# A two-layer transformer kernel on one Trainium2 core: one regular timetable for the 192 modulation adds in place of hand-set places

## The reference

```
mod = jax.nn.silu(c) @ w_ada[l] + b_ada[l]          # (1, 2048) @ (2048, 12288)
shift_a, scale_a, gate_a, shift_f, scale_f, gate_f = jnp.split(mod, 6, axis=-1)
h = rms_norm(x, g_attn_pre[l]) * (1.0 + scale_a[:, None]) + shift_a[:, None]
...                                                 # projections, two attentions, w_o
x = x + gate_a[:, None] * rms_norm(mixed, g_attn_post[l])
h = rms_norm(x, g_ffn_pre[l]) * (1.0 + scale_f[:, None]) + shift_f[:, None]
ff = (jax.nn.silu(h @ w_gate[l]) * (h @ w_up[l])) @ w_down[l]
x = x + gate_f[:, None] * rms_norm(ff, g_ffn_post[l])
```

## Time and profile before

| | |
|---|---|
| median of 3 runs | 2756.78 us (2755.45 to 2757.07) |
| the profiled execution's own time | 2756.78 us, of which 2755.0 us are the span from the first to the last instruction |
| PE busy | 2618.4 us, 95% of the span |
| DVE busy | 1839.9 us, 67% |
| ACT busy | 1313.6 us, 48% |
| DMA | 558.31 MB, mean 203 GB/s |
| PE on the chain that ended last | 91% |
| mean granted TensorE clock | 0.966 of full |
| L1297, 180 of the 192 adds | 1278 ns each |

### The profile page before, as it was taken

The page is one execution under the profiler, slowest core; times in us unless marked ns, Lnnn a source line. Parts: engine busy times, 40 slices in busy tenths (PEclk is TensorE's granted clock), DMA queues, the critical chain, the costliest instruction groups (busy, mean ns, idle before and its releaser), DMA issues.

```text
span 2755.0 us, 36683 instructions
## 1 busy us (share of the span) xinstructions
PE 2618.4 (95%) x14858; PEld 2265.9 (82%) x14858; DVE 1839.9 (67%) x2620; ACT 1313.6 (48%) x2021; POOL 0.2 (0%) x4
## 2 busy tenths in 40 slices
PE   7999769999999999999998999869799999999998
PEld 6887658888888888888887888658688888888886
DVE  5566455677878788788788546774666656655555
ACT  5456254445544444444445443455554444444454
POOL 0000000000000000000000000000000000000000
PEclk9999689999999999999999999969899999999999
DMA  7555006677878878878785654304377757655552
GB/s 256 192 197 170 1 31 215 206 251 276 294 241 277 285 259 293 271 268 305 254 277 186 199 187 154 117 0 138 107 244 239 235 185 231 227 183 195 187 189 86
DMA packets 329857, 558.31 MB, mean 203 GB/s; under 512 B 13526, under 2 KB 158128, under 8 KB 329176
## 3 DMA queue, kind: packets, MB, share of 16 engines
q1 hardware_dynamic: 299312, 451.58, 49.8%
q10 hardware_dynamic: 30376, 104.39, 10.9%
HBM read 551.72 MB, written 4.19 MB: 202 GB/s over the span
## 4 chain that ended last, share of the span: by engine, by line
PE 91%; DVE 4%; ACT 2%; issue 1%; ACTq 0%; DVEq 0%
PE ps L441 56%; PE ps L442 29%; PE ps L521 1%; PE ps L458 1%; PE ps L532 1%; PE ps L509 1%; DVE sm_cols L1419 1%; PE ps L728 1%; PE ps L636 0%; ACT wh L829 0%; DVE wl L1281 0%; PE ps L476 0%; PE ps L650 0%; PE ps L497 0%; DVE ts L1792 0%
## 5 line engine op out<-in xcount | busy, mean ns | idle before, releaser
L441 PE MATMUL ps<-hs,wh 128*128 128x512 f32 x4816 | 1685.0, 395 | 18.6 <-issue 12.3
L1281 DVE TENSOR_TENSOR wl<-raw,wh 128x1024 fp32r<-128x1024 f32 x856 | 1039.5, 1223 | 766.4 <-ACT wh L829 763.4
L829 ACT ACTIVATE wh<-raw 128x1024 fp32r<-128x1024 f32 x856 | 899.1, 1059 | 1134.6 <-PE ps L442 1102.0
L442 PE MATMUL ps<-hs,wl 128*128 128x256 f32 x4816 | 1345.2, 279 | 0.0
L441 PEld LDWEIGHTS ps<-hs,wh 128*128 128x128 f32 x4816 | 903.8, 188 | 232.4 <-issue 15.7
L442 PEld LDWEIGHTS ps<-hs,wl 128*128 128x128 f32 x4816 | 909.1, 189 | 1.2 <-issue 1.2
L441 PE MATMUL ps<-ff,wh 128*128 128x512 f32 x1728 | 606.7, 396 | 0.0
L442 PE MATMUL ps<-ff,wl 128*128 128x256 f32 x1728 | 484.8, 281 | 0.0
L441 PEld LDWEIGHTS ps<-ff,wh 128*128 128x128 f32 x1728 | 324.1, 188 | 76.5
L442 PEld LDWEIGHTS ps<-ff,wl 128*128 128x128 f32 x1728 | 326.7, 189 | 0.0
L855 ACT ACTIVATE te<-ps 128x256 f32<-128x256 f32 x445 | 132.9, 383 | 9.8 <-PE ps L442 6.2
(11 more groups left out here) (238 smaller groups left out, 1314.6 us busy)
## 6 DMA issues: line engine op xcount, KB each, us to landing
raw<-w_down SPq DMA_DIRECT2D x108, 1024.0 KB
raw<-w_in SPq DMA_DIRECT2D x80, 1024.0 KB
raw<-w_up SPq DMA_DIRECT2D x64, 1024.0 KB
ada_w<-w_ada ACTq DMA_DIRECT2D x96, 512.0 KB, 5.1
ada_more<-w_ada ACTq DMA_DIRECT2D x96, 512.0 KB, 5.8
raw<-w_gate SPq DMA_DIRECT2D x88, 512.0 KB
raw<-w_up SPq DMA_DIRECT2D x88, 512.0 KB
raw<-w_in SPq DMA_DIRECT2D x68, 512.0 KB
```

Source lines behind the costliest of these rows:

```text
L441: nc.tensor.matmul(ps[0:m, b, :], wh[:, slot, w0:w0 + m], x2, start=k == 0, stop=False)
L442: mm = nc.tensor.matmul(ps[0:m, b, 0:T], wl[:, slot, w0:w0 + m], x2[:, 0:T], start=False, stop=end)
L829: nc.scalar.activation(wh[:, h % WH_SLOTS, :], raw[:, slot, HALF * q:HALF * (q + 1)], ACT.Copy).then_inc(wh_ready, 1)
L1281: nc.vector.tensor_tensor(wl[:, h % WH_SLOTS, :], raw[:, slot, HALF * q:HALF * (q + 1)], wh[:, h % WH_SLOTS, :], ALU.subtract).then_inc(wl ...
```

## The change

The hand-set places are replaced by one pattern for all 12 chunks. A chunk now spans four steps. Counted as (step of the chunk, half), its adds stand after (-1,6), that is half 6 of the step before, then (0,0) (0,2) (0,4) (0,6), (1,0) (1,2) (1,4) (1,6), (2,0) (2,2) (2,4) (2,6), (2,7), (3,0) and (3,1). The sum stands after half 3 of step 3, the close after the feed of half 5. The chunks lie in LGY's gate steps 4 to 7, the four steps of L4, the 32 of LF1 (an up chunk and a down chunk in each quarter), and steps 1 to 8 of LF2's first part, where chunks 10 and 11 now both lie. The sum writes bank 0 of the next step's banks, not bank 3, and the wait for the close moves from that step's fourth tile to its start; one wait is added ahead of the sums of squares after LF1.

```
--- before.py
+++ after.py
@@ -78,32 +78,31 @@
 
 
 
-
-
-def ada_places(panel, *halves):
-
-    return [2 * panel + h for h in halves]
-
-
-ADA_PLACES = [ada_places(LGY.panel + 24, 1, 4, 7, 10, 13, 16, 19, 22, 25, 28, 31, 34, 37, 40, 43, 46),
-              ada_places(L4.panel, 4, 5, 7, 8, 10, 12, 14, 15, 16, 18, 20, 22, 24, 26, 28, 30)]
-ADA_STEPS = [(L4.panel, L4.step, 2), (LF1.panel, LF1.step, 2)]
-for c in range(4):
-    up, t_up = LF1.panel + 32 * c, LF1.step + 8 * c
-    ADA_PLACES += [ada_places(up, 4, 5, 7, 11, 13, 15, 19, 21, 23, 27, 29, 31, 32, 33, 34, 35),
-                   ada_places(up + 20, 0, 1, 3, 5, 6, 8, 10, 11, 13, 14, 16, 17, 18, 20, 21, 22)]
-    ADA_STEPS += [(up + 16, t_up + 4, 6), (up + 32, t_up + 8, 2)]
-for c in range(2):
-    ADA_PLACES.append(ada_places(LF2.panel + 4 + 44 * c, *[8 * s + h for s in range(8) for h in (2, 5)]))
-    ADA_STEPS.append((LF2.panel + 36 + 44 * c, LF2.step + 9 + 11 * c, 2))
-ADA_ADDED = {ADA_PLACES[m][k]: 16 * m + k for m in range(12) for k in range(16)}
+ADA_STEPS = ([LGY.panel + 6 * s for s in range(4, 8)] + [L4.panel + 4 * s for s in range(4)]
+             + [LF1.panel + 4 * s for s in range(32)] + [LF2.panel + 4 * s for s in range(1, 9)])
+ADA_PLACES = [(-1, 6)] + [(s, h) for s in range(3) for h in (0, 2, 4, 6)] + [(2, 7), (3, 0), (3, 1)]
+ADA_SUMS, ADA_CLOSES = 3, 5
+
+
+def ada_half(chunk, step, h):
+
+    first = ADA_STEPS[4 * chunk] if step < 0 else ADA_STEPS[4 * chunk + step]
+    if step < 0:
+        first -= 6 if chunk == 0 else 4
+    return 2 * first + h
+
+
+ADA_ADDED = {ada_half(m, *ADA_PLACES[k]): 16 * m + k for m in range(12) for k in range(16)}
 ADA_LAST = 2 * LF2.panel + 2
 ADA_LOADED = {2 * (LGY.panel + 12) + 1: [0, 1, 2, 3], ADA_LAST: [160, 161, 162, 163]}
 for at_half, n in ADA_ADDED.items():
     if n + 4 < 160 or 164 <= n + 4 < 192:
         ADA_LOADED.setdefault(at_half + 1, []).append(n + 4)
-ADA_SUMMED = {2 * ADA_STEPS[m][0] + ADA_STEPS[m][2]: m for m in range(12)}
-ADA_BEFORE = {ADA_STEPS[m][0] + 4: m for m in range(12)}
+ADA_SUMMED = {ada_half(m, 3, ADA_SUMS): m for m in range(12)}
+ADA_CLOSED = {ada_half(m, 3, ADA_CLOSES): m for m in range(12)}
+ADA_BEFORE = {ADA_STEPS[4 * m + 3] + 4: m for m in range(12)}
+ADA_BANKS = ([LGY.step + 15, L4.step + 4] + [LF1.step + 4 * m + 4 for m in range(8)]
+             + [LF2.step + 5, LF2.step + 9])
 RAW_SLOTS = 4
 PANEL_INC = 64
 N_VECTORS = 15
@@ -423,6 +422,8 @@
 
 
                 pe.wait_ge(tile_summed, 4 * (t + dt) + 4)
+                if p + dp in ADA_BEFORE:
+                    pe.wait_ge(ada_read, ADA_BEFORE[p + dp] + 1)
                 last = len(tiles) - 1
                 for h in range(2 * panels):
                     slot = (2 * p + h) % WH_SLOTS
@@ -431,8 +432,6 @@
                     pe.wait_ge(wl_ready, 2 * (p + dp) + h + 9)
                     for n, (c0, m) in enumerate(tiles):
                         b = bank(t, n)
-                        if h == 0 and n == 3 and p + dp in ADA_BEFORE:
-                            pe.wait_ge(ada_read, ADA_BEFORE[p + dp] + 1)
                         for kk in range(2):
                             k = 2 * h + kk
                             end = k == 4 * panels - 1
@@ -455,7 +454,7 @@
                 pe.wait_ge(tile_summed, 4 * (t + dt) + 4)
                 pe.wait_ge(ada_used, 16 * chunk + 20)
                 for j in range(8):
-                    mm = nc.tensor.matmul(ps[:, bank(t, 3), j:j + 1], ada_acc[:, j * P:(j + 1) * P], ones[:, 0:1],
+                    mm = nc.tensor.matmul(ps[:, bank(t, 0), j:j + 1], ada_acc[:, j * P:(j + 1) * P], ones[:, 0:1],
                                           start=True, stop=True)
                 mm.then_inc(ada_summed, 1)
 
@@ -715,6 +714,7 @@
             ffn_chunk(0, first=True)
             for c in range(1, 4):
                 ffn_chunk(c)
+            pe.wait_ge(ada_read, 10)
             norm_sums(NORM_A, L7.step)
 
 
@@ -1281,10 +1281,10 @@
                 nc.vector.tensor_tensor(wl[:, h % WH_SLOTS, :], raw[:, slot, HALF * q:HALF * (q + 1)],
                                         wh[:, h % WH_SLOTS, :], ALU.subtract).then_inc(wl_ready, 1)
                 at_half = h + 2 * dp - 4
-                if at_half in ADA_SUMMED:
-                    ada_close(ADA_SUMMED[at_half])
                 if at_half in ADA_ADDED:
                     ada_add(ADA_ADDED[at_half] // 16, ADA_ADDED[at_half] % 16)
+                if at_half in ADA_CLOSED:
+                    ada_close(ADA_CLOSED[at_half])
 
             def ada_add(chunk, k):
 
@@ -1300,7 +1300,7 @@
 
             def ada_close(chunk):
                 dve.wait_ge(ada_summed, chunk + 2)
-                nc.vector.tensor_tensor(mod[:, 8 * chunk:8 * chunk + 8], ps[:, bank(ADA_STEPS[chunk][1] + 1, 3), 0:8],
+                nc.vector.tensor_tensor(mod[:, 8 * chunk:8 * chunk + 8], ps[:, bank(ADA_BANKS[chunk], 0), 0:8],
                                         bada[:, 8 * chunk:8 * chunk + 8], ALU.add).then_inc(ada_read, 1)
 
             def total(t, dt, n, dst, m=P, inc=1):
```

## The result

The changed kernel takes 2802.2 us (median of 6 runs, 2782.8 to 2806.4), the kernel before 2756.9 in the same comparison (2754.1 to 2767.8). All ratios here, with their 95% intervals, are over the fast runs alone, and one run of the kernel before in a later comparison, 3308.1 us at a granted clock of 0.735, is left out. The ratio is 1.0139 (1.0115 to 1.0162), some 38 us; the two medians lie 45 us apart, more than that, since four of the six runs of the kernel before took 2754 to 2757 us and two 2766 to 2768. The forecast was 2771.6 with a range of 2763 to 2782: the sign was right, but of the 38 to 45 us it had 15. The profiled execution took 2795.55 us, its span is 2793.8 us against 2755.0.

A forecast was written before the change was run, and what follows sets the result against it. TensorE was taken to set the time, new waits being paid in full. 2756.8 us plus 14.8 of stalls at the sums, with pace and clock at 0, gave 2771.6 us; range 2763 to 2782.

The forecast's parts named there:

- TensorE sets the time, a new wait is paid in full; what is only moved costs nothing.: Feed-forwards: TensorE busy 95% of the span, so only its new waits cost; moved adds, loads and closes cost 0.
- The wait for `ada_read`: At the next step's start: the moved wait costs nothing, as the close stands after half 5's feed.
- The stalls.: TensorE waits at sums for the last add: up chunks 11.8, LF2 1.9, L4 0.9, down 0.2; together 14.8 us.
- The full clock through the stalls: At the new waits ahead of sums: the granted clock stays full, adding 0 us to the forecast.
- a rival at 20 in 100: Up chunks' stalls and sums: the clock falls, 1.5 to 2.1 us each, 6 to 8 together, giving 2779; 20 in 100.
- The pace.: TensorE's two speeds, 22.19 and 22.61 us a step, with borders at sums: taken as 0, range -7 to +8 us.
- a slow half: Half of a step at TensorE's slower pace, 0.053 us longer; 197 counted between sums, 10.5 us.
- the rule that each sum turns the pace over as before: LF1 would have 4 x 32 slow halves for 109, LF2 32 for 88: 2.0 us less.
- The rival on the other side: All slow stretches vanish as the sums move: -10.5 us, giving 2761.1, +0.16%; 7 in 100.
- The rival with late feeds: Up steps: denser adds delay `wl` for half 4, up to 1 us in each of 16 steps, giving 2785; 4 in 100.
- the marks I named: Profile signs: longest four waits 2.9 to 3.0 us, last add at +13.9; wrong if new clock falls between 760 and 1485 us.
- The step of 27.0 us: Quarter 1's steps with a sum: 22.19 + 1.8 for the sum + 3.0 for the stall = 27.0 us.

The follow-up runs named there:

- sum5: The changed kernel with its 12 sums after half 5 of their step, not half 3; all adds stay. 2762.9 us, ratio 0.9997 to the kernel before.
- add25: The changed kernel with one add of each chunk moved from after half 7 of the third step to after half 5. 2772.9 us, ratio 1.0039.
- before_s5: The kernel before with the sums of its four up chunks after half 5 of the first down step, not half 6. 2778.3 us, ratio 1.0054.
- after_b: The changed kernel, unaltered, run and profiled again. 2801.9 us, ratio 1.0133 to the kernel before.
- busy12: The changed kernel with 12 extra unused matmuls ahead of the sum's wait in each of the four up chunks. 2787.2 us, ratio 1.0082.
- busy_all: The changed kernel with extra unused matmuls ahead of the sum's wait: 12 in each up chunk, 4 in each LF2 chunk. 2789.7 us, ratio 1.0083.
- before_b: The kernel before, unaltered, profiled once more in another execution. 2763.3 us in one run.
- before_c: The kernel before, unaltered, profiled as a third draw, on the same chip as the second. 2769.5 us in one run.

## Why the prediction was right in kind and wrong in size

- **TensorE sets the time, a new wait is paid in full; what is only moved costs nothing.** Right: sum5 has every add, load and close moved and is at 0.9997. The wait for `ada_read` cost nothing.
- **The stalls.** Right, place by place: the up chunks 2.76 to 2.97 us (2.96 forecast), LF2 0.74 and 0.95 (0.94), L4 0.89 (0.9), the down chunks 0.1 in all (0.2), LGY none. Together 14.4 against 14.8. They could be read from a kernel that didn't have them, because the same queue stood once per quarter in it. That was not luck: for add25 and before_s5 the same count gave 1.8 and 2.1 us, and the stalls were 1.55 to 1.78 and 1.76 to 2.08.
- **The full clock through the stalls: this step failed.** I had the fall as a rival at 20 in 100 and chose against it, since the sums alone, 1.7 us of single columns, had never brought one. That holds (none of 36 sums in three executions of the kernel before, none of 12 in sum5), but doesn't answer for a stall ahead of a sum. Of the sums that TensorE waited for idle, those after 2.2 us or more brought falls in 20 of 20 (none of the four up chunks in either busy kernel, where it worked); 1.5 to 2.1 us in 8 of 8; 0.7 to 1.0 us in 7 of 10 (changed 2 of 3, after_b 2 of 3, busy12 3 of 3, busy_all 0 of 1 at L4); 0.2 us in 1 of 2; 0.1 us in none of 5. The term was also mis-sized. I priced a fall by the restarts in the earlier trace rows, which stay at half clock for 3.0 and 4.1 us, at 1.5 to 2.1. It was 1.6 or 3.2, since in four of the six falls the clock stayed at half for 6.8 us, in the sum (1.7 slowed to as much as 3.4) or in the pairs behind it; and there were six, not four, as the stalls of 0.7 to 1.0 us count. So the measured term is 16.1 us, in place of 0 in the forecast, or of the rival's 6 to 8.
 The Trainium skill (TensorE: Matmul & The Clock Gate, Part 1: The HAM clock gate) gave the direction, an idle TensorE is put back to half rate, and busy12 agrees: with the array at work no fall at four stalls of the same length.
- **The pace.** The size of a slow half (0.053 us) was right, and so was the place of the borders at sums and stops. Wrong was the rule that each sum turns the pace over as before: in sum5 LF1 is slow only until its first up chunk's sum, where by the rule every other 32 halves would be. And it isn't set by the program alone. I took its term as 0 with -7 to +8 for this change; against the first profile of the kernel before it was +3.5 us in one execution of the changed kernel and +15.7 in the other, and three executions of the unchanged kernel alone span 12.8 us. The range was too narrow for that.
- **The rival on the other side,** in which the pace pays the loss back, didn't come: it was 3.5 us against, and no draw of the pace seen here would have paid for the 30 us of stalls and clock. The rival with late feeds didn't come: the longest wait for `wl` is 0.6 us.
- **Of the marks I named,** the four waits of 2.9 to 3.0 us (the profile counts them to 2.8) and the add at +13.9 are there. The step of 27.0 us took 30.2 to 30.4 in three of the four quarters, 28.8 in the last. The falls between 760 and 1485 us, which I had named as what would prove me wrong, came.

## What to carry to other kernels

A reduction that one engine issues for another's accumulation must be placed by the last add's end in time, read at the step where the helper's queue is longest, not by counting slots; two halves (5.5 us) of room on TensorE were the difference between no loss and 1.4%. When a wait on TensorE is added next to work that streams few columns, price it at more than its length: here 14.4 us of stalls brought a loss of 16.1 us to the clock. Where a stall can't be moved, matmuls put into it keep the clock, as they did (with products that nothing uses) at all ten places where it was tried; and before a small difference is argued, profile the unchanged kernel more than once.

## What the runs showed of the hardware that I had not expected

- The granted clock fell after short pauses: with an idle stretch of 1.5 to 2.1 us and 1.7 us of one-column matmuls behind it in 8 of 8 cases, with 0.7 to 1.0 us in 7 of 10, with 0.2 us in 1 of 2. With full-width products behind, 0.7 to 1.8 us of idle time brought none in 30 cases. A fall cost about 1.6 or 3.2 us.
- TensorE has two paces in the same loop at full clock and without waits, 22.19 and 22.61 us a step (0.3467 and 0.3533 us a pair). One lasts until the next interruption (a sum, a stop), up to some 194 halves here, and differs between executions of one program, also on one chip (393 and 468 slow halves in before_b and before_c). What sets it stays open. I tried nothing that would choose it. By the table, as an estimate, a kernel that was always quick would take some 2743 us of span.
